# Who squares, scales and turns the activations where one sub-layer hands over to the next, in a two-layer fp32 trunk kernel

## The reference, cut to what matters

```python
for l in range(DEPTH):
    mod = c_act @ ada_w[l] + ada_b[l]
    sh_m, sc_m, g_m, sh_f, sc_f, g_f = jnp.split(mod, 6, axis=-1)
    h = modulate(rmsnorm(x, mix_pre_g[l]), sh_m, sc_m)
    y = mixer_sublayer(h, ...)
    x = x + g_m[:, None, :] * rmsnorm(y, mix_post_g[l])
    h = modulate(rmsnorm(x, ffn_pre_g[l]), sh_f, sc_f)
    y = conv_glu(h, ffn_w_up[l], ffn_conv_w[l], ffn_conv_b[l], ffn_w_down[l])
    x = x + g_f[:, None, :] * rmsnorm(y, ffn_post_g[l])
```

## Time and profile before

| | us |
|---|---|
| median of 3 runs (932.42 to 935.62) | 934.29 |
| the profiled execution | 934.45 |
| its span, first to last instruction | 932.6 |
| PE busy | 909.3 (98% of the span) |
| DVE busy | 731.4 (78%) |
| ACT busy | 535.4 (57%) |
| POOL busy | 86.2 (9%) |
| mean granted PE clock | 0.994 of full |

### The profile page before, as it was taken

The page is one execution under the profiler, slowest core; times in us unless marked ns, Lnnn a source line. Parts: engine busy times, 40 slices in busy tenths (PEclk is TensorE's granted clock), DMA queues, the critical chain, the costliest instruction groups (busy, mean ns, idle before and its releaser), DMA issues.

```text
span 932.6 us, 16982 instructions
## 1 busy us (share of the span) xinstructions
PE 909.3 (98%) x6752; PEld 853.8 (92%) x6752; DVE 731.4 (78%) x988; ACT 535.4 (57%) x715; POOL 86.2 (9%) x162
## 2 busy tenths in 40 slices
PE   6899999999999999999999999999999999999997
PEld 5799999999978999999979999999998799999996
DVE  4889888888787887886886887898789686666765
ACT  4456866555358555554673585954555764555554
POOL 0122202000001020000001220200000100000000
PEclk9799999999999999999999999999999999999999
DMA  9889867666883677776645986867668365556451
GB/s 363 295 258 311 278 220 247 226 204 213 326 284 110 221 257 256 258 245 203 197 147 168 256 292 205 267 200 262 217 221 298 106 221 186 180 184 212 137 188 46
DMA packets 135132, 209.06 MB, mean 224 GB/s; under 512 B 5536, under 2 KB 104224, under 8 KB 135072
## 3 DMA queue, kind: packets, MB, share of 16 engines
q1 hardware_dynamic: 120960, 162.73, 53.1%
q0 software_dynamic: 13824, 45.36, 13.5%
q10 hardware_dynamic: 288, 0.14, 0.0%
HBM read 204.28 MB, written 1.05 MB: 220 GB/s over the span
## 4 chain that ended last, share of the span: by engine, by line
PE 85%; DVE 5%; ACT 4%; DMA 3%; issue 2%; DVEq 0%; ACTq 0%; SPq 0%
PE banks L1808 79%; DVE w_lo L1168 2%; DMA raw<-in_w_in 2%; ACT w_hi L640 1%; PE banks L2079 1%; DMA adw<-in_ada_rows 1%; PE banks L1929 1%; DMA cst<-shape_constants 1%; PE banks L2086 1%; PE banks L1948 1%; DVE EF L1710 1%; PE banks L2095 1%; DVE adw L1161 1%; ACT h_hi L698 0%; ACT AB L867 0%
## 5 line engine op out<-in xcount | busy, mean ns | idle before, releaser
L1808 PE MATMUL banks<-h_lo,w_hi 128*128 128x256 f32 x1504 | 423.5, 282 | 2.1 <-DVE h_lo L1229 2.1
L1808 PE MATMUL banks<-h_hi,w_lo 128*128 128x256 f32 x1504 | 419.9, 279 | 0.0
L1808 PE MATMUL banks<-h_hi,w_hi 128*128 128x256 f32 x1504 | 419.8, 279 | 0.0
L1808 PEld LDWEIGHTS banks<-h_lo,w_hi 128*128 128x128 f32 x1504 | 282.6, 188 | 5.8 <-issue 4.3
L1808 PEld LDWEIGHTS banks<-h_hi,w_lo 128*128 128x128 f32 x1504 | 282.7, 188 | 0.9
L1808 PEld LDWEIGHTS banks<-h_hi,w_hi 128*128 128x128 f32 x1504 | 282.6, 188 | 0.0
L1168 DVE TENSOR_TENSOR w_lo<-raw,w_hi 128x2048 fp32r<-128x2048 f32 x96 | 219.5, 2288 | 32.2 <-ACT w_hi L640 31.2
L640 ACT ACTIVATE w_hi<-raw 128x2048 fp32r<-128x2048 f32 x96 | 182.6, 1911 | 97.6 <-PE banks L1808 77.3
L1710 DVE SCALAR_TENSOR_TENSOR EF<-banks,par,EF 128x254 f32<-128x254 f32 (+1 forms) x176 | 76.8, 477 | 57.3 <-ACT EF L1020 52.5
L1734 DVE TENSOR_TENSOR w_lo<-raw,w_hi 128x2048 fp32r<-128x2048 f32 x42 | 96.0, 2285 | 21.5 <-ACT w_hi L1039 21.5
L1039 ACT ACTIVATE w_hi<-raw 128x2048 fp32r<-128x2048 f32 x42 | 80.3, 1913 | 36.7 <-PE banks L1808 36.7
(11 more groups left out here) (281 smaller groups left out, 1238.7 us busy)
## 6 DMA issues: line engine op xcount, KB each, us to landing
raw<-in_w_in SPq DMA_DIRECT2D x52, 1024.0 KB, 6.7
raw<-in_ffn_w_up SPq DMA_DIRECT2D x44, 1024.0 KB, 5.0
adw<-in_ada_rows POOLq DMA_DIRECT2D x80, 512.0 KB, 5.6
raw<-in_ffn_w_down SPq DMA_DIRECT2D x22, 1024.0 KB, 4.9
raw<-in_w_out SPq DMA_DIRECT2D x8, 1024.0 KB, 8.3
raw<-in_ret_wo SPq DMA_DIRECT2D x4, 1024.0 KB, 6.0
raw<-in_lru_wo SPq DMA_DIRECT2D x4, 1024.0 KB, 5.1
raw<-in_mla_wo SPq DMA_DIRECT2D x4, 1024.0 KB, 7.3
```

Of the source, the lines that this page charges most:

```text
L1808: ins = MM(ps, lhs, rhs, start=first and n == 0, stop=last and n == 2)
```

## The change: what it does

- Squares: for chunk 1 at each seam, DVE squares the second half of x and sums it (a new `square` on DVE, semaphore n_sx), right behind the residual; ACT keeps the first half, and its new `other_half` waits for n_sx and takes the Sqrt.
- Chunk 0 inside a layer: ACT modulates all four tiles of half 0 (two of them from `DVE_BANK`); DVE none of that half.
- Chunk 1 at all three seams: no diagonal. DVE multiplies x by the reciprocal into `normed` (in `tmp`), in two halves of 512 features, each with a count of n_dg, and PE turns its tiles by eight plain transposes; `to_features` waits for each half. Chunk 0, and both chunks at the start of the kernel, keep the diagonal.
- Order on DVE, inside a layer: `inverse_rms` of chunk 1 comes ahead of `modulate(.., 0, 1)`, and both modulations of chunk 1 ahead of both `h_low`. Between the layers: `modulate(.., 0, 1)` and `inverse_rms` come ahead of `split_block(l2, 1)`.
- Between the layers, `h_low` of chunk 0, half 1 moves from DVE to POOL, and `v_product(0, 1)` waits for it (n_lo0).
- `gate_rows` of the MLP also waits for ACT's modulation of chunk 0.

```diff
--- before.py
+++ after.py
@@ -312,9 +312,10 @@
...
-        n_ss, n_pt, n_sq, n_rs, n_dg = sig("n_ss", 8), sig("n_pt", 4), sig("n_sq", 4), sig("n_rs", 4), sig("n_dg", 4)
+        n_sx = sig("n_sx", 2)
+        n_ss, n_pt, n_sq, n_rs, n_dg = sig("n_ss", 8), sig("n_pt", 4), sig("n_sq", 4), sig("n_rs", 4), sig("n_dg", 8)
         n_tp, n_ha, n_hd, n_hi, n_lo = (sig(n, 8) for n in ("n_tp", "n_ha", "n_hd", "n_hi", "n_lo"))
-        n_lo0 = sig("n_lo0", 2)
+        n_lo0 = sig("n_lo0", 3)
...
@@ -372,6 +373,8 @@
...
+        normed = tmp[:].rearrange("p a b -> p (a b)")[:, 0:D]
         ACT_BANK, DVE_BANK = ((4, 5), (0, 1)), ((6, 7), (3, 2))
@@ -547,10 +550,10 @@
                     pool.wait_ge(ada_red.s, n - 1)
                     load(n, n % 2)
-            def h_low(l, half):
+            def h_low(l, n, half):
                 cs, ks = slice(0, P), slice(4 * half, 4 * half + 4)
-                pool.wait_ge(n_hi.s, n_hi.at(l, 5 + half))
+                pool.wait_ge(n_hi.s, n_hi.at(l, h_step(l, n, 0, half)))
                 nc.gpsimd.tensor_tensor(h_lo[:, ks, cs], h32[:, ks, cs], h_hi[:, ks, cs].bitcast(F32), ALU.subtract).then_inc(n_lo0.s, 1)
@@ -583,7 +586,7 @@
                 next_tiles(t + 12, t + NT)
                 next_tiles(t + NT, min(t + NT + DK + 2, TILES))
                 for half in range(2):
-                    h_low(l, half)
+                    h_low(l, 2, half)
                 next_tiles(t + NT + DK + 2, min(t + 2 * NT - 12, TILES))
                 if l + 1 < L:
                     pool.wait_ge(s_ps.s, s_ps.at(l, 4))
@@ -591,6 +594,8 @@
                     pool.wait_ge(wbd_zero, l + 2)
                     recurrence_weights(l + 1)
                 next_tiles(t + 2 * NT - 12, min(t + 2 * NT + 2, TILES))
+                if l + 1 < L:
+                    h_low(l + 1, 0, 1)
 
@@ -680,13 +685,20 @@
                     act.wait_ge(n_pt.s, n_pt.at(l, n + 1))
                     A_(st[:, 2 + c:3 + c], sums[:, 0, c, 1:2], ACT.Sqrt, scale=1.0 / D, bias=part[:, 0, c:c + 1]).then_inc(n_sq.s, 1)
-            def modulate(l, n, c, half):
+            def other_half(l, n, c):
+                act.wait_ge(n_sx.s, n_sx.at(l, n // 2))
+                act.sem_inc(n_ss.s, 1)
+                act.wait_ge(n_pt.s, n_pt.at(l, n + 1))
+                A_(st[:, 2 + c:3 + c], sums[:, 0, c, 1:2], ACT.Sqrt, scale=1.0 / D, bias=part[:, 0, c:c + 1]).then_inc(n_sq.s, 1)
+            def modulate(l, n, c, half, tiles=2):
                 cs = slice(P * c, P * c + P)
                 act.wait_ge(n_tp.s, n_tp.at(l, 2 * n + half + 1))
-                for i in range(2):
-                    k = 4 * half + i
-                    a = A_(h32[:, k, cs], PS[:, ACT_BANK[c][half], P * i:P * i + P], ACT.Identity,
+                for i in range(tiles):
+                    k, bank = 4 * half + i, (ACT_BANK if i < 2 else DVE_BANK)[c][half]
+                    a = A_(h32[:, k, cs], PS[:, bank, P * (i % 2):P * (i % 2) + P], ACT.Identity,
                            scale=hscale[:, k:k + 1], bias=mod[:, k:k + 1])
                 a.then_inc(n_ha.s, 1)
@@ -729,9 +741,9 @@
                 post_square(l, ph, 1, 1)
                 act.wait_ge(mod_ready.s, mod_ready.at(l, ph + 2))
                 if ph == 0:
-                    modulate(l2, n, 0, 0)
+                    modulate(l2, n, 0, 0, 4)
                     square(l2, n + 1, 1, 0)
-                    square(l2, n + 1, 1, 1)
+                    other_half(l2, n + 1, 1)
                     h_high(l2, n, 0, 0)
                     modulate(l2, n, 0, 1)
                     h_high(l2, n, 0, 1)
@@ -1202,7 +1214,12 @@
                 dve.wait_ge(n_sq.s, n_sq.at(l, n + 1))
                 V.reciprocal(st[:, 4 + c:5 + c], st[:, 2 + c:3 + c]).then_inc(n_rs.s, 1)
                 dve.wait_ge(n_rs.s, n_rs.at(l, n + 1))
-                V.tensor_scalar(diag[:, c, :], ident, st[:, 4 + c:5 + c], None, ALU.mult).then_inc(n_dg.s, 1)
+                if c == 0 or n == 1 and l == 0:
+                    V.tensor_scalar(diag[:, c, :], ident, st[:, 4 + c:5 + c], None, ALU.mult).then_inc(n_dg.s, 2)
+                    return
+                for half in range(2):
+                    cols = slice(512 * half, 512 * half + 512)
+                    V.tensor_scalar(normed[:, cols], x[:, c, cols], st[:, 4 + c:5 + c], None, ALU.mult).then_inc(n_dg.s, 1)
             def shift_scale(l, ph):
@@ -1258,6 +1275,13 @@
                     y = (CD, AB)[c][:].rearrange("p a b -> p (a b)")[:, cols]
                     V.scalar_tensor_tensor(x[:, c, cols], y, st[:, 10 + c:11 + c], x[:, c, cols], ALU.mult,
                                            ALU.add).then_inc(x_ready.s, 1)
+            def square(l, n, c, half):
+                cols = slice(512 * half, 512 * half + 512)
+                dve.wait_ge(x_ready.s, x_ready.at(l, 2 * n + half + 1))
+                V.scalar_tensor_tensor((lat, tmp)[c][:].rearrange("p a b -> p (a b)")[:, cols], x[:, c, cols], 1.0, x[:, c, cols],
+                                       ALU.mult, ALU.mult, accum_out=sums[:, 0, c, half:half + 1]).then_inc(n_sx.s, 1)
             def half_end(l, ph, first):
@@ -1281,13 +1305,14 @@
                 dve.wait_ge(mod_ready.s, mod_ready.at(l, ph + 2))
                 if ph == 0:
                     residual(l, ph, 1)
-                    modulate(l2, n2, 0, 0)
+                    square(l2, n2 + 1, 1, 1)
+                    dve.sem_inc(n_hd.s, 1)
+                    inverse_rms(l2, n2 + 1, 1)
                     modulate(l2, n2, 0, 1)
-                    inverse_rms(l2, n2 + 1, 1)
                     dve.sem_inc(n_lo.s, 2)
                     modulate(l2, n2 + 1, 1, 0)
+                    modulate(l2, n2 + 1, 1, 1)
                     h_low(l2, n2 + 1, 1, 0)
-                    modulate(l2, n2 + 1, 1, 1)
                     h_low(l2, n2 + 1, 1, 1)
                     split_block(l2, first + 1)
                 else:
@@ -1295,10 +1320,11 @@
                     residual(l, ph, 1, (0,))
                     h_low(l2, n2, 0, 0)
                     residual(l, ph, 1, (1,))
+                    square(l2, n2 + 1, 1, 1)
+                    modulate(l2, n2, 0, 1)
+                    inverse_rms(l2, n2 + 1, 1)
                     split_block(l2, 1)
-                    inverse_rms(l2, n2 + 1, 1)
-                    modulate(l2, n2, 0, 1)
-                    h_low(l2, n2, 0, 1)
+                    dve.sem_inc(n_lo.s, 1)
                     modulate(l2, n2 + 1, 1, 0)
                     modulate(l2, n2 + 1, 1, 1)
                     h_low(l2, n2 + 1, 1, 0)
@@ -1816,12 +1842,16 @@
             def to_features(l, n, c):
-                pe.wait_ge(n_dg.s, n_dg.at(l, n + 1))
                 for half in range(2):
+                    pe.wait_ge(n_dg.s, n_dg.at(l, 2 * n + half + 1))
                     for k in range(4):
                         kk = 4 * half + k
                         bank, i = (ACT_BANK if k < 2 else DVE_BANK)[c][half], k % 2
-                        ins = MM(PS[:, bank, P * i:P * i + P], x[:, c, P * kk:P * kk + P], diag[:, c, :], start=True, stop=True)
+                        ps, ks = PS[:, bank, P * i:P * i + P], slice(P * kk, P * kk + P)
+                        if c == 0 or n == 1 and l == 0:
+                            ins = MM(ps, x[:, c, ks], diag[:, c, :], start=True, stop=True)
+                        else:
+                            ins = nc.tensor.transpose(ps, normed[:, ks], ident)
                     ins.then_inc(n_tp.s, 1)
@@ -1887,6 +1917,8 @@
                     j = J[("v", i)]
                     ready(l, j)
                     pe.wait_ge(n_lo.s, n_lo.at(l, h_step(l, c, c, i)))
+                    if l > 0 and (c, i) == (0, 1):
+                        pe.wait_ge(n_lo0.s, n_lo0.at(l, 0))
                     wh, wl = weights(l, j)
                     for k in range(4):
                         kk = 4 * i + k
@@ -2240,6 +2272,7 @@
                 to_features(l, 3, 1)
                 pe.wait_ge(n_hd.s, n_hd.at(l, 6))
+                pe.wait_ge(n_ha.s, n_ha.at(l, 6))
                 gate_rows(l, 1, 0, 6)
                 gate_rows(l, 1, 1, 7)
                 s_g, s_u, s_d = (at_slot(l, NM + 2 + part) for part in range(3))
```

## The result

| | before | after |
|---|---|---|
| median of 9 runs | 933.13 us | 936.95 us |
| lowest to highest | 932.42 to 935.62 | 934.57 to 939.97 |
| span of the profiled execution | 932.6 | 936.2 |

The ratio is 1.0039, 95% interval 1.0027 to 1.005: slower by 3.8 us, against a forecast of 1.0 us less.

What follows compares the result with a forecast made beforehand. PE was 98% busy, so time could come only from its waits at the seams. Two inner seams saving 0.76 in all plus 0.26 between the layers gave 1.02 us less, 934.29 to 933.3 us; range 931.8 to 937.8.

Steps and rivals of the forecast that it cites:

- The steps inside a layer: Inner seams: up projection starts 0.24 later but is dense from 293.08 instead of 293.46, saving 0.38 us per seam.
- Rival D: Chunk 1's scalings take 0.69 each, so inner seams become dense at 293.52; +0.3, 934.6 us; chance 0.10.
- The 1.0 us saved on PE ... alone it is worth nothing: Turning chunk 1 by plain transposes saves 1.0 us on PE, wholly in time in which PE then waits.
- Rival C: Clock falls at inner seams, each costing 3.1 us: 936.4 us with one, 939.5 with both; chance 0.12.
- hidden under the split: Between the layers: POOL's low part runs 485.15 to 486.42 during DVE's split; values (0, 1) start at 487.13, 0.26 us saved.
- rival A: Between the layers, POOL's subtraction must wait for DVE's split; values (0, 1) start 1.02 us later, 934.6 us; chance 0.25.
- Rival B: Inside a layer, POOL gets in before DVE's second scaling; +0.96 us per seam, 937.2 us; chance 0.08.
- within 0.3%: Whole kernel: time changes by less than 0.3%, 2.8 us, not told from none; chance given as 0.78.
- faster: Whole kernel: faster by over 0.3%, only through something not seen; chance given as 0.06.

Runs made afterwards that it cites:

- e1: Changed kernel, with POOL's subtractions at the two inner seams also waiting for DVE's second scaling; 936.44 us, ratio 1.0046.
- e2: Changed kernel, with PE's idle time at the seams filled by more constant matmuls; 934.17 us, ratio 1.0012 against the kernel before.
- e5: Changed kernel with e1, e2 and e3 together; 933.23 us, ratio 0.9999 against the kernel before.
- e7: Change at the two inner seams only, with POOL's wait and inner fillers; between the layers as in the kernel before; 932.55 us, ratio 0.9993.
- e4: Changed kernel, with chunk 1 turned by eight fp32 matmuls by the identity instead of eight plain transposes; 934.18 us, ratio 1.0014.
- e9: Changed kernel, with the diagonal and fp32 matmuls for chunk 1 at all seams instead of scaling and plain transposes; 932.30 us, ratio 0.9985.
- e10: e9 with chunk 0's second low part between the layers back on DVE behind the split of block 1; 931.70 us, ratio 0.9985.
- e3: Changed kernel, with chunk 0's second low part between the layers back on DVE and no PE wait for POOL; 936.71 us, ratio 1.0041.
- e8: e7 with DVE's modulation (0, 1) put between the two scalings of chunk 1; 933.02 us, ratio 0.9994.

## Why the prediction was wrong

- *The steps inside a layer* held. The first matmul was foreseen 8.97 behind the seam's start and came at 9.06; the stop is gone; ACT stood idle 0.44 for DVE's modulation; the pair of scalings was foreseen at 0.89 and took 0.88; the square took 0.70 with the read. Where neither a fall nor POOL interfered, the stretch is 0.2 to 0.5 shorter (e1, e2, e5, e7), 0.38 foreseen. Rival D is refuted.
- *"The 1.0 us saved on PE ... alone it is worth nothing"* is the step that failed. It is worth less than nothing: it takes busy time away from a seam that had kept its clock. From 287.10 to 291.40 PE was busy 3.00 of 4.30 us before, and 2.04 of 4.50 after, and the clock fell there. Giving PE work back at the seams, useful or not, brought 2.8 us (e2, e4). Rival C had the mechanism and a chance of 0.12. By the Trainium skill, TensorE: Matmul & The Clock Gate, "Part 4: PE-mode transpose", it became the likely one. The falls agree with that rule, but it is not shown: e4 does not separate it from the shorter busy time, and the falls in e9 and e10 came without transposes.
- C's price was too high: 3.1 us from the prologue's fall, 1.71 measured. Its place was too narrow: the seam between the layers, where the sum had 2.8 us with nothing but eight transposes (484.37 to 487.13), was not counted, and the clock fell there in after, e1 and e3.
- *POOL's low part "hidden under the split"* is the second step that failed, as rival A said: values (0, 1) started 10.38 behind the seam's start, with 10.57 foreseen for A and 9.29 for the forecast. With the low part on DVE behind the split the start was 9.86 (e3, e5). The Trainium skill, SBUF — State Buffer, "Who interferes with whom", describes it, and the trace agrees: 2.99 for 1.27 beside the split.
- Rival B happened in layer 1 alone, in every profile that had the scalings and no wait (after, e2, e3, e4: 1.92 each). It costs 0.90 (layer 1's stretch, e1 against after), 1.34 foreseen.
- A, B and C were given chances as if one excluded the others. They lie in different places and add up: +1.1 against the forecast (A, 10.38 for 9.29), +0.9 (B in one layer) and +2.8 for the clock (e2 against after). With the forecast's -1.0 that is +3.8, and 3.8 was measured. That it agrees to a tenth is luck, since each term is uncertain by some tenths.
- The forecast started from 934.29, the median of three runs; nine runs of the same kernel gave 933.13. That 936.95 lies inside the range of 931.8 to 937.8 owes something to this: with every bound 1.16 lower the range would have ended at 936.6.
- The chances don't add up as written. By its own terms "within 0.3%" is 0.81 and "faster" 0.03, not 0.78 and 0.06; nothing hangs on it.

What decides in a given execution at which seam the clock falls stays open: layer 1's seam, with the longest idle time in sum (0.67, 0.72 and 1.81), kept it in the profiled execution. Open too is whether a transpose does less for the clock than a matmul of the same length.

## What to carry to other kernels

Time saved on TensorE in a stretch in which it then waits is not free: it can cost the clock, and here a few constant matmuls, or the slower form of an operation, bought it back. Before work is moved to GpSimd, look at what VectorE reads from SBUF beside it; both directions of waiting cost. Mechanisms that lie in different places belong in one sum, not in rival cases.

## What the runs showed of the hardware

- VectorE and GpSimd wait for each other where both read SBUF: a 1.27 us GpSimd subtraction took 2.99 beside a VectorE subtraction of 2.29, a pair of VectorE scalings 1.92 instead of 0.88 with one GpSimd subtraction between them, and a VectorE subtraction 1.48 instead of 0.69 when it asked during a GpSimd one (e8). Beside VectorE's reads of PSUM the GpSimd subtraction kept its 1.27.
- A fall of the granted clock lasted 3.41 us at half speed, 1.71 us of full clock, in all six cases between 35 and 900 us of a span: four at seams (after, e1, e3) and two late in the prologue, behind 2.38 and 2.57 us of idle time (e9, e10).
- The granted clock's column says 1.00 before its first change, also where PE runs slower. PE's prologue in the kernel before and in the changed one:

```profile
16.41 2.09 PE L1868 MATMUL banks<-ccol,raw 128*128 128x1 f32 x16
```

```profile
16.51 3.41 PE L1898 MATMUL banks<-ccol,raw 128*128 128x1 f32 x16
```

The same sixteen instructions, both at 1.00 by the column. So whether a mean clock is near 0.993 or near 0.999 says first of all whether PE was fast early in the prologue and fell at about 23 us, which the column shows, or was slow from the start, which it doesn't. The kernel before has both, at the same time (932.57 us at 0.993, 932.56 at 0.999). It also has executions at 0.991 and 0.992, which took 933.9 to 935.6 us: it too seems to lose the clock once more in some, at a place that no profile of it shows.
